# Mixture-of-experts step: summing and norming tokens slot by slot inside the expert stage

## The reference, cut to what matters

```
h = x + mix(x)                              # residual rows
for each token: two experts of one group, weights sw
y[token] = sum over its two experts of sw * (silu(xn @ w_gate[e]) * (xn @ w_up[e])) @ w_down[e]
out = rms_norm(h + y, final_norm_g)         # the last step
```

## Time and profile before

| | us |
|---|---|
| median of 3 runs | 1157.05 |
| lowest, highest | 1151.5, 1157.98 |
| the profiled execution, own time | 1157.81 |
| its span, first to last instruction | 1156.0 |

### The profile page before, as it was taken

How to read it: one execution, slowest core, us unless ns; L and a number is a source line. 1 busy time by engine, 2 the same in 40 slices (tenths; PEclk the granted TensorE clock), 3 DMA queues, 4 the chain that set the end, 5 groups by cost and what they waited for, 6 DMA issues and landing times. The chain is left out here.

```text
span 1156.0 us, 16386 instructions
## 1 busy us (share of the span) xinstructions
PE 1061.8 (92%) x6188; PEld 721.7 (62%) x6188; DVE 570.6 (49%) x1275; ACT 412.9 (36%) x975; POOL 241.7 (21%) x298
## 2 busy tenths in 40 slices
PE   6999989999997999999997998799999999999980
PEld 3643334444454777777785565487878787878860
DVE  4406699999987866666846551314111111111114
ACT  2325534878454545455631333211111111111114
POOL 4741116643411000000004210011212121212110
PEclk9999989999995999999998899799999999999995
DMA  8600000010192311111011761599999999999928
...
DMA packets 51342, 191.42 MB, mean 166 GB/s; under 512 B 10926, under 2 KB 13950, under 8 KB 41029
## 3 DMA queue, kind: packets, MB, share of 16 engines
...
...
q10 hardware_dynamic: 158, 0.16, 0.1%
...
## 5 line engine op out<-in xcount | busy, mean ns | idle before, releaser
L1562 PEld LDWEIGHTS ps<-mem 128*128 128x128 f32 x2048 | 236.5, 194 | 16.8 <-issue 16.8
L1562 PE MATMUL ps<-mem 128*128 128x96 f32 x2048 | 235.9, 277 | 0.8 <-DVE mem L2577 0.8
L1638 ACT ACTIVATE mem<-ps 128x512 f32<-128x512 f32 (+7 forms) x340 | 150.1, 480 | 229.2 <-PE ps L1355 62.1
L2136 DVE TENSOR_SCALAR_CACHE_REDUCE mem<-mem 128x768 bf16<-128x768 f32 (+2 forms) x134 | 166.5, 1286 | 0.0
L1403 PE MATMUL ps<-mem 128*128 128x256 f32 x512 | 118.3, 384 | 1.9 <-DVE mem L2425 1.1
L1568 PE MATMUL ps<-mem 128*96 128x512 f32 x256 | 117.6, 602 | 2.5 <-DVE mem L2569 2.5
L2569 DVE TENSOR_TENSOR mem<-mem,ps 128x192 f32<-128x192 f32 x32 | 11.4, 355 | 212.8 <-ACT mem L2012 212.8
L1022 POOL DMA_INDIRECT h_rows<-mem x32 | 46.5, 1454 | 295.9 <-DVE mem L2584 295.9
L1403 PEld LDWEIGHTS ps<-mem 128*128 128x128 f32 x512 | 95.8, 192 | 15.9 <-DVE mem L2441 2.4
L2012 ACT ACTIVATE mem<-ps 128x192 f32<-128x192 f32 x32 | 10.6, 332 | 262.5 <-PE ps L1562 262.5
L1568 PEld LDWEIGHTS ps<-mem 128*96 128x96 f32 x256 | 39.0, 162 | 57.1 <-issue 51.2
...
...
## 6 DMA issues: line engine op xcount, KB each, us to landing
...
```

What stands on the lines that cost most here:

```text
L1562: ins = mm(ps[:, 2 + s, j * CAP:(j + 1) * CAP], wgu[w][:, j // 2, k, (j % 2) * P:(j % 2 + 1) * P], xgT[:, s, k, :], start=(k == 0), stop=( ...
L1638: return fn(out, in_, ACT.Copy, scale=scale)
L2136: v.tensor_scalar(bufs[a % 3][0:R, 0:w], sc, mid[:, a:a + 1], None, ALU.is_ge, ALU.add, accum_out=cnt[:, a:a + 1]).then_inc(step, 1)
```

## The change

No row is added into `h_rows` any more. Of a token's two experts, the one with the lower number (or block) is its first, the other its last. The first expert's result is stored as a plain row in a new DRAM tensor, `first_expert_rows`. When the last expert of a token is due, POOL gathers the token's residual row and its stored first result into the slot (`hg`, 4 buffers, and `rg`, 2 buffers); DVE adds both and the expert's own output; ACT squares and takes the root (`spread`), DVE norms (`norm_out`), and POOL scatters the finished row straight to the output (`finished`, one scatter for prompt rows and one for sample rows). Each of these comes some experts late in its engine's order: DVE sums e-1 and norms e-2, ACT squares e-2, POOL sends e-3. For every table the rows that do not concern a slot get an index beyond the tensor, which `bounds_check` with `oob_is_err=False` leaves out. Which of the two is last travels through the one-hot products as a quarter subtracted from the token number, so DVE's table work grows (`later_ones`, `targets`). The new tensor is cleared at the start of phase 2b. The row gathers of xn are issued three experts ahead instead of two, first in each round. The reload, the nine-tile norm and the plain stores at the end are gone. Waits on landed stores stand in the overflow branch alone. Some semaphores are shared between phases, and the final gamma is loaded between the weights of experts 2 and 3.

The core of the diff (the overflow branches, the constants and the sharing of semaphores are left out):

```diff
-OQ = 4
+HRING = 4
+FAR_ROW = 8192.0
...
-        hc = cut(TILES * D, (TILES, D))
-        sq = cut(D // 2, None, BF16)
+        hg = cut(HRING * D, (HRING, D))
+        rg = cut(2 * D, (2, D))
...
-        h_dram = nc.dram_tensor("h_rows", (NTOK + CAP, D), F32, kind="Internal").ap()
+        h_dram = nc.dram_tensor("h_rows", (NTOK, D), F32, kind="Internal").ap()
+        r_dram = nc.dram_tensor("first_expert_rows", (NTOK, D), F32, kind="Internal").ap()
...
-            sp.dma_start(h_dram[NTOK:NTOK + CAP].rearrange("p (c n) -> p c n", n=P),
-                         zrow[0:CAP].unsqueeze(1).broadcast_to([CAP, D // P, P])).then_inc(pads_cleared, 16)
+            for i in range(TILES):
+                sp.dma_start(rowsof_dram(r_dram, i).rearrange("p (c n) -> p c n", n=P),
+                             zrow[0:rows(i)].unsqueeze(1).broadcast_to([rows(i), D // P, P])).then_inc(first_cleared, 16)
...
             weights(2, 2)
+            sp.dma_start(gb[:, :], final_norm_g.rearrange("(a n) -> a n", a=1).partition_broadcast(P)).then_inc(gn_in, 16)
             weights(3, 3)
...
-            sp.dma_start(gb[:, :], final_norm_g.rearrange("(a n) -> a n", a=1).partition_broadcast(P)).then_inc(gn_in, 16)
...
-            sp.wait_ge(experts_done, 1)
-            for s in range(2):
-                sp.wait_ge(eo_out[s], 16 * (NE // 2))
-            for i in range(TILES):
-                if i >= OQ:
-                    sp.wait_ge(hc_in[i % OQ], 16 * (i // OQ))
-                sp.dma_start(hc[0:rows(i), i, :], rowsof_dram(h_dram, i)).then_inc(hc_in[i % OQ], 16)
-            for i in range(TILES):
-                store_y(sp, i)
-            sp.wait_ge(y_out, 16 * TILES)
+            for s in range(HRING):
+                sp.wait_ge(y_out[s], 32 * (NE // HRING))
...
+            def gathered(rows_, src, table, e, last_row, done):
+                pool.indirect_dma_start(rows_, None, src, bass.IndirectOffsetOnAxis(ap=table[0:CAP, e:e + 1], axis=0),
+                                        bounds_check=last_row, oob_is_err=False).then_inc(done, 16)
+            def scattered(dst, table, e, last_row, rows_, done):
+                pool.indirect_dma_start(dst, bass.IndirectOffsetOnAxis(ap=table[0:CAP, e:e + 1], axis=0), rows_, None,
+                                        bounds_check=last_row, oob_is_err=False).then_inc(done, 16)
             def rows_of(e):
                 if e >= 2:
                     pool.wait_ge(xT_filled[1], e - 1)
-                pool.indirect_dma_start(xg[0:CAP, e % 2, :], None, xn_dram,
-                                        bass.IndirectOffsetOnAxis(ap=slot_tok[0:CAP, e:e + 1], axis=0)).then_inc(xg_in[e % 2], 16)
-
-            def add_rows(e, out_rows, done):
-                pool.indirect_dma_start(h_dram, bass.IndirectOffsetOnAxis(ap=slot_dst[0:CAP, e:e + 1], axis=0),
-                                        out_rows, None, compute_op=ALU.add).then_inc(done, 16)
+                gathered(xg[0:CAP, e % 2, :], xn_dram, slot_tok, e, NTOK - 1, xg_in[e % 2])
+            def finished(e):
+                pool.wait_ge(y_ready, e + 1)
+                s = e % HRING
+                scattered(y_rows[0], slot_last, e, SEQ - 1, hg[0:CAP, s, :], y_out[s])
+                scattered(y_rows[1], slot_late, e, SR - 1, hg[0:CAP, s, :], y_out[s])
             rows_of(0)
             rows_of(1)
             tiles_out(pool, h_out, TILES)
-            pool.wait_ge(pads_cleared, 16)
+            pool.wait_ge(first_cleared, 16 * TILES)
             pool.wait_ge(targets_ready, 1)
+            rows_of(2)
             for e in range(NE):
-                if e + 2 < NE:
-                    rows_of(e + 2)
+                if e + 3 < NE:
+                    rows_of(e + 3)
+                if e >= 3:
+                    finished(e - 3)
+                if e:
+                    pool.wait_ge(eo_out[(e - 1) % 2], 16 * ((e - 1) // 2 + 1))
+                if e >= 2:
+                    pool.wait_ge(fin_ready, e - 1)
+                gathered(rg[0:CAP, e % 2, :], r_dram, slot_last, e, NTOK - 1, rg_in[e % 2])
+                if e >= HRING:
+                    pool.wait_ge(y_out[e % HRING], 32 * (e // HRING))
+                gathered(hg[0:CAP, e % HRING, :], h_dram, slot_last, e, NTOK - 1, hg_in[e % HRING])
+                if e == NE - 1:
+                    finished(e - 2)
+                    finished(e - 1)
+                    finished(e)
                 for c in range(2):
                     pool.wait_ge(dn_emptied[c], e + 1)
-                if e:
-                    pool.wait_ge(eo_out[(e - 1) % 2], 16 * ((e - 1) // 2 + 1))
-                add_rows(e, ob[0:CAP, e % 2, :], eo_out[e % 2])
-            for s in range(2):
-                pool.wait_ge(eo_out[s], 16 * (NE // 2))
+                scattered(r_dram, slot_first, e, NTOK - 1, ob[0:CAP, e % 2, :], eo_out[e % 2])
...
+                    act.wait_ge(fin_ready, e - 1)
                 copy(ob[0:CAP, s, 0:512], ps[0:CAP, 5, :], scale=slot_w[0:CAP, e:e + 1]).then_inc(dn_emptied[0], 1)
+            def spread(e):
+                s = e % 2
+                act.wait_ge(fin_ready, e + 1)
+                if e >= 2:
+                    act.wait_ge(y_ready, e - 1)
+                fn(sq[0:CAP, :], hg[0:CAP, e % HRING, :], ACT.Square, accum_out=ssq3[0:CAP, s:s + 1]).then_inc(ssq3_ready, 1)
+                act.wait_ge(ssq3_ready, e + 1)
+                fn(std3[0:CAP, s:s + 1], ssq3[0:CAP, s:s + 1], ACT.Sqrt, scale=1.0 / D, bias=const("eps", CAP)).then_inc(std3_ready, 1)
             def experts(q, last=False):
                 for u in range(WSLOTS):
                     silu(q, u)
                     if u < WSLOTS - 1 or not last:
                         keep_xgT(q, u + 1) if u < WSLOTS - 1 else keep_xgT(q + 1, 0)
+                    if q * WSLOTS + u == NE - 1:
+                        spread(NE - 3)
+                        spread(NE - 2)
                     keep_out(q, u)
+                    if 2 <= q * WSLOTS + u < NE - 1:
+                        spread(q * WSLOTS + u - 2)
             keep_xgT(0, 0)
             experts(0)
             for q in range(1, NE // WSLOTS - 1):
                 experts(q)
             experts(NE // WSLOTS - 1, last=True)
+            spread(NE - 1)
...
-            act.drain().then_inc(experts_done, 1)
-            fn(stat[:, 254:255], const("z"), ACT.Sqrt)
-            for i in range(TILES):
-                r, s = rows(i), i % 2
-                act.wait_ge(hc_in[i % OQ], 16 * (i // OQ + 1))
-                if i:
-                    act.wait_ge(std3_ready, i)
-                fn(sq[0:r, :], hc[0:r, i, :], ACT.Square, accum_out=ssq3[0:r, i:i + 1]).then_inc(ssq3_ready, 1)
-                act.wait_ge(ssq3_ready, i + 1)
-                fn(std3[0:r, i:i + 1], ssq3[0:r, i:i + 1], ACT.Sqrt, scale=1.0 / D, bias=const("eps", r)).then_inc(std3_ready, 1)
...
+            def later_ones(tiles, r):
+                ef, rk, key, later = (x[0:r, tiles, :] for x in (EF, RK, KEY, LATER.unsqueeze(2)))
+                link(v.tensor_scalar(key, rk, float(CAP), float(NE), ALU.is_ge, ALU.mult))
+                link(v.tensor_tensor(key, key, ef, ALU.add))
+                link(v.tensor_tensor(later, key[:, :, 1:2], key[:, :, 0:1], ALU.is_gt))
+                v.tensor_scalar(QUARTER[0:r, 1, tiles], LATER[0:r, tiles], 0.25, None, ALU.mult)
+                link(v.tensor_scalar(QUARTER[0:r, 0, tiles], LATER[0:r, tiles], -0.25, 0.25, ALU.mult, ALU.add))
...
             def targets():
-                link(v.tensor_scalar(slot_pad, slot_sum, 0.0, const("pad", CAP)[:, 0:1], ALU.is_equal, ALU.mult))
-                v.scalar_tensor_tensor(out=slot_dst[0:CAP, 0:NE], in0=slot_sum, scalar=-1.0, in1=slot_pad, op0=ALU.add, op1=ALU.add)\
-                    .then_inc(targets_ready, 1)
+                link(v.tensor_scalar(slot_sum, slot_sum, -1.0, float(NTOK), ALU.mult, ALU.add))
+                dve.wait_ge(slots_ready, 1)
+                link(v.tensor_copy(slot_row, slot_tok[0:CAP, 0:NE]))
+                link(v.tensor_tensor(slot_sum, slot_sum, slot_row, ALU.subtract))
+                v.scalar_tensor_tensor(out=slot_first[0:CAP, 0:NE], in0=slot_sum, scalar=4 * FAR_ROW, in1=slot_row, op0=ALU.mult, op1=ALU.add)
+                link(v.tensor_scalar(slot_sum, slot_sum, 0.0, FAR_ROW, ALU.is_equal, ALU.mult))
+                link(v.tensor_tensor(slot_row, slot_row, slot_sum, ALU.add))
+                v.tensor_copy(slot_last[0:CAP, 0:NE], slot_row)
+                link(v.tensor_scalar(slot_sum, slot_row, float(SEQ), FAR_ROW, ALU.is_lt, ALU.mult))
+                v.scalar_tensor_tensor(out=slot_late[0:CAP, 0:NE], in0=slot_row, scalar=-float(SEQ), in1=slot_sum, op0=ALU.add, op1=ALU.add)
+                dve.drain().then_inc(targets_ready, 1)
...
                     slots(i)
+                    later_ones(slice(i, i + 1), r)
                     weigh(i)
                     for n in range(2):
```

(46 more changed lines are left out.)

124 lines of the change are left out of this document (84 added, 40 removed).

## The result

The changed kernel takes 1179.94 us in the median of 4 runs (1173.82 to 1182.65), the kernel before 1157.06 beside it: a ratio of 1.0206, 95% interval 1.0173 to 1.0238. It is slower, by about 2%, where 1145 us was forecast, and outside the range of 1138 to 1161.

What follows compares the result with a forecast made beforehand. PE was taken to bound the expert stage, unchanged at 11.61 us per expert; a shorter end at 1142.4 plus 1.3 and 0.5 gave 1144.2 against 1156.0, 11.8 gained, so 1145 us from the 1157.05 median; range 1138 to 1161.

Steps and rivals of the forecast that it cites:

- the landing in POOL's part: Expert stage: the scatter of first results, 34 rows per expert without addition, lands in 6.7 us; ends 4.6 and 10.1.
- The transfers have 15 us in hand: Expert stage: DMA engines are full but ahead of PE, last weights through by about 1096, their product from 1111.3.
- the prediction's own loop: POOL in the expert stage: scatter, landing L, reaction, two gathers, L + 0.77 + 2.46; fits 11.61 us up to L = 8.4.
- The bytes: Expert stage: 3888 KB per expert against 3840, 4 us later at the end at 341 GB/s, hidden in the 15.
- Skipped rows: Expert stage: out-of-bounds rows taken to cost nothing; upper end, each costing a moved row, 126 us slower, outside the range.
- DVE: Expert stage: two additions, reciprocal and scaling at 1.28 us per long operation, done at a+9.6 with 2.5 us to spare.
- POOL: Expert stage: six indirect DMAs, gathers 0.93 and scatters 1.45 us each, gaps 0.30, together 8.9 us in 11.61.
- Rival 1: Expert stage: POOL's loop becomes the period if landing stays at 9.3; 7 us net slower, 1164 us; chance 0.13.
- Rival 2: Expert stage: POOL issues nothing during DVE's two-operand operations, 3 x 1.28 us per expert; 13 net slower, 1170 us; chance 0.05.
- Rival 3: Expert stage, ACT: a table load waits with its silu; 38 us lost, 1183 us; chance 0.02.
- Rival 4: Program end: only half as short, landings of 8 to 9 us, last store near 1148; 1150 us; chance 0.14.
- the end: After silu of expert 31: last sums, norms and stores finish at 1142.4 against 1156.0; ends 1138.5 and 1149.

Runs made afterwards that it cites:

- e5: Changed kernel with DVE's sums moved behind the product PE waits for, and POOL's gathers issued ahead of its stores: 1178.85 us.
- e3: Changed kernel loading only half of each expert's weights from the fifth expert on, all products kept: 1148.63 us, single run.
- e11: Changed kernel with first results added into h_rows and sample rows finished as one tile after the last expert, four indirect transfers per expert: 1146.43 us.
- e15: e13 plus two gathers per expert into a buffer nobody reads, 32 of 96 rows in bounds: 1203.13 us.
- e16: e13 plus two gathers per expert into a buffer nobody reads, 68 of 96 rows in bounds: 1251.4 us.
- e17: Kernel before plus one gather of 68 rows per expert, all moved, into a buffer nobody reads: 1244.45 us.
- e14: e13 plus two gathers per expert into a buffer nobody reads, every row out of bounds: 1149.88 us.
- e10: Changed kernel with DVE's overflow destinations moved from between experts 3 and 4 to behind the first expert's product: 1175.12 us.
- e7: Kernel before plus four scatters of 96 entries per expert, every row out of bounds: 1163.8 us.
- e13: e11 with only the overflow destinations moved behind the first expert's product: 1141.12 us, ratio 0.9871 to the kernel before.
- e2: Changed kernel with both gathers, sum, norm and stores one expert later and a third output buffer: 1186.3 us.
- e9: Changed kernel scattering first results into another tensor than the one gathered from, without POOL's wait for that landing: 1187.57 us.
- e8: Changed kernel with all traffic kept, but DVE's additions take other operands, so DVE does not wait for gathered rows: 1163.26 us.

## Why the prediction was wrong

**The step that failed** is that POOL's new row traffic was let pass for almost nothing. Its first half is the landing in POOL's part: "Scaling only the loaded part, 5.2 + 4.1 x 34/96 = 6.7 us." Measured 9.0 for the scatter, 7.4 to 8.6 for the other five. The loaded part is not the transfer's own rows; it is the traffic around it, which stayed: with half the weights the same scatter took 5.8. Its second half is "The transfers have 15 us in hand": the earlier trace rows show a DMA share of 1.03 at 341 GB/s, and the slack was read from the weights. It is true of the weights, which are asked for four experts ahead, and says nothing of rows that must be there within one. The landing alone does not make the 35 us: with 9.0 in it the prediction's own loop, 9.0 + 0.77 + 2.46 = 12.2 us, costs 0.6 x 28 - 6 = 11, and e5 had a landing of 6.6 and kept the time. What the runs showed in its place is the row traffic as a whole beside the weights: the stage comes back from 407.1 to 377.3 us with half the weights (e3), and to 376.7 with four transfers in place of six and 4.7 MB less (e11).

**The bytes** were costed at 4 us, hidden, by the rate of 341 GB/s. The sum itself, 48 KB more per expert (28 of them 1.4 MB), was near the 1.63 MB that the queue's row shows. The price was wrong: 5.1 and 6.4 us per MB of rows in e15 and e16, POOL's added waits included, and 10.0 in e17. e14 and e10 agree with the lower prices: as many transfers and entries, overflow destinations first in both, 4.71 MB less and 25.2 us faster, 5.4 us per MB. Of the 35 us, 1.63 MB come to 8 to 10, by e17 to 16. Such prices are from other kernels, and their sum with those below is an account, not a measurement.

**Skipped rows** were taken at nothing. No row of theirs moved, as assumed, but they are packets of transfers that POOL has to issue: 7.1 us for 384 entries per expert in the kernel before (e7), 8.8 for 192 in e13 (e14). The upper end of 126 us was far off, so leaving that end out of the range was right, but nothing was not the value: for the 372 per expert here it is 7 to 17 us.

**DVE**: additions 1.22, scaling 1.28, done within the expert where the rows are there, as forecast. What the sum left out is the block of overflow destinations, once, 9.1 us long: a stall of 7.8 us against 1.7 and slow matmuls behind it; moving it gained 5.3 us between e11 and e13.

**POOL**: a scatter without addition occupies it for 0.96 us, not 1.45, which made up for nothing, since POOL was not short of time.

**The rivals.** Rival 1 named the right symptom, the landing staying near 9, and the right side, but its mechanism fell in e2 and e9, and its 1164 us were 16 short: it counted one loop where the whole queue was behind. Rival 2 did happen, at a small part of its size. Two places of the changed kernel:

```profile
923.08 1.28 DVE L2677 SCALAR_TENSOR_TENSOR mem<-mem 96x1024 f32<-96x1024 f32 x1
923.18 2.03 POOL L1012 DMA_INDIRECT mem<-first_expert_rows,mem  x1 [5.34 <-DMA first_expert_rows<-mem]
...
986.98 1.23 DVE L2659 TENSOR_TENSOR mem<-mem 96x1024 f32<-96x1024 f32 x1 [0.17 <-DMA mem<-h_rows,mem]
...
988.05 1.00 POOL L1012 DMA_INDIRECT mem<-first_expert_rows,mem  x1 [1.53 <-DMA first_expert_rows<-mem]
988.24 1.22 DVE L2666 TENSOR_TENSOR mem<-mem 96x1024 f32<-96x1024 f32 x1
```

The first gather begins while DVE's scaling has 1.18 us to go and ends 0.85 us after it; the second begins with 0.16 us to go, and the addition that starts behind it does not hold it. Of the 190 indirect transfers from 745 us on, 18 began with over 0.3 us of such an operation ahead of them and were held, taking 1.23 to 2.03 us and ending 0.79 to 0.86 us after the operation; two that began within 0.03 us of the operation's start were not held, and the 140 that began outside one took at most 1.00. The 18 cost POOL some 14 us in all, where the rival reckoned 3.84 per expert, and they do not carry the loss: e8 has 21 transfers over 1.6 us, against 13 here, and is 17 us faster. The Trainium skill, GPSIMD Engine Reference, Key points, says that POOL contends with DVE instructions with two SBUF inputs; for transfers that begin during one the trace agrees. Rival 3: each table load stands ahead of its silu's wait, as forecast. Rival 4: the end gained 10.2 us of the 13.6 forecast. Moved by the 35.0 us that silu 31 is late, the steps hold: first addition forecast 1162.9, found 1161.64; last scaling done 1168.0, found 1168.0; last store issued 1172.5, found 1171.52. The transfers there land within 2.2 to 3.9 us, the last by 1174.9. What fills the time to 1180.8 is a step that the sum did not have, POOL's drain at the end of its program (source view of L137):

```profile
L137 POOLq DRAIN  x1: 7412/7412/7412, 1173.2 to 1173.2; - x1
```

It is 7.4 us long and begins when POOL has issued its last transfer. Before, that drain began at 1131.4, took 5.3 us and lay beside the reload.

**Right**, or near, were the stage's start (PE began at 744.14, forecast some 1.8 us late, found 0.5 early), the hidden clearings and table loads, and that the end is worth about 10 us. That the end's steps come out to the microsecond while it lacks POOL's drain is partly luck: POOL's scatters were reckoned 0.5 us too long. All this is small beside the stage.

**What stays open**: how POOL's queue and the weights' share the engines, packet by packet, and so whether it is the engines or POOL's one queue that has no room: in the changed kernel's windows of 50 us in which PE stood still the share was 0.82 to 0.94. No run shows what part of the prices in e15 to e17 is POOL's own wait for the added gathers; one without that wait would tell. Nor was it tried to give the rows precedence over the weights. Almost every size was put too low: e15, e16 and e17 came out above their ranges.
